# Late picks' last steps on GpSimd, and the first eight row gathers behind their own slots

## The chip, the cores and the metric

The kernel runs on one core of one Trainium2 chip. The metric is the device time of one execution in microseconds (us). TensorE multiplies matrices, VectorE and ScalarE work element by element, GpSimd here issues gathers (DMAs whose rows are chosen by an index in SBUF) and does a little element work, SyncE issues the plain loads. All are ordered only by semaphores.

## The reference

The program is two transformer-like blocks over 256 tokens of width 2048, all in fp32. The change lies in the last part of the second block, a product-key expert layer:

```python
def peer_ffn(h, w_pq, peer_keys, peer_u, peer_v):
    q = jnp.einsum("bsd,dhk->bshk", h, w_pq).reshape(B, S, PEER_HEADS, 2, KEY_DIM)
    sub = jnp.einsum("bshpk,hpnk->bshpn", q, peer_keys).astype(jnp.float32)
    s, i = lax.top_k(sub, PEER_TOPK)                       # 16 best of 128, for two key sets
    cand = (s[..., 0, :, None] + s[..., 1, None, :]).reshape(B, S, PEER_HEADS, PEER_TOPK * PEER_TOPK)
    cidx = (i[..., 0, :, None] * N_KEYS + i[..., 1, None, :]).reshape(...)
    top_s, pos = lax.top_k(cand, PEER_TOPK)                # 16 best of the 256 sums
    idx = jnp.take_along_axis(cidx, pos, axis=-1)          # the experts
    gate = jax.nn.softmax(top_s, axis=-1)
...
        u = jnp.take(peer_u, i_blk, axis=0)
        a = jax.nn.gelu(jnp.einsum("td,thkd->thk", x_blk, u)) * g_blk
        v = jnp.take(peer_v, i_blk, axis=0)
        return jnp.einsum("thk,thkd->td", a, v)
```

There are 8 heads, 16 experts for each token and head, and 16384 experts with a row of 2048 numbers (8 KB) in each of the tables u and v.

## The kernel before

Tokens lie on the 128 partitions, in two halves. A **unit** is one head of one half: 16 units, 16 picks each, so 256 **gathers** in all. A gather fetches for each of 128 tokens one row of u: 128 rows of 8 KB, 1 MB. It lands in one of eight slots (`GR = 8`) of the tile `expert_rows`. For each gather VectorE runs one **dot** (L2195), the product of the row and the normed token `h2`, summed over 2048 elements. Dot n releases slot n % 8 (semaphore `freed`), and GpSimd's gather n + 8 waits for that; so eight gathers at most are issued or landed and not yet used. GpSimd runs its instructions in the order written.

What experts a unit picks is worked out by VectorE in three **parts**, in the list `PICK_PARTS`. `best_keys` finds the 16 best of 128 keys, twice. `best_pairs` finds the 16 best of the 256 sums and splits each position into two places. `experts_of_pairs` (L1776 to L1790) turns places into experts: it compares places with a row of numbers (`one_hot`, 2 x 16 x 16), multiplies by the key numbers `best_f`, sums over the last 16 into `keys_of`, and makes the index, `keys_of[0] * 128 + keys_of[1]`, cast to an integer. Then it increments `picked`, and the gathers of that unit may go.

Units 0 to 3 are picked in the stage before (`out_and_queries_stage`), between VectorE's halves of the weight split (L194). The 12 late units are picked between the dots of the gather stage (`peer_stage`): 36 parts spread over the first 232 dots (`PICK_DOTS`), so one part behind every sixth or seventh dot, and a unit's three parts take 19.33 dots. Third parts stand behind dots 19, 38, 57, 77, 96, 115, 135, 154, 173, 193, 212 and 231; the next part behind them follows 6 dots later in 4 cases (19, 77, 135, 193) and 7 dots later in 7.

The first eight gathers are issued at the end of `out_and_queries_stage`. Slots 0 to 3 lie where the four-slot ring of weight slabs was, slots 4 to 7 where the high and low halves of the split weights were. Behind dot 236 VectorE makes the indices of the next phase (`index_pieces`). When all dots are done, the v phase begins: gathers of half rows of v on one side, and slabs of v multiplied by TensorE on the other. Its first six slab loads (L2107) start when dot 248 is done.

Of the kernel before, what the change touches and what calls it, by code (L numbers as in the profile page):

```python
# [23 lines left out]
ALU = mybir.AluOpType  # L24
AX = mybir.AxisListType

P = 128
# [17 lines left out]
PH, NKEYS, TOPK = 8, 128, 16  # L45
PICKS = PH * TOPK
RING = 4
KPE_W = 256
GR = 8
# [3 lines left out]
C_ID, C_NA, C_CAUSAL, C_TRIL, C_FREQ, C_IOTA = 0, 128, 384, 512, 640, 672  # L53
# [49 lines left out]
class Core:  # L103
# [33 lines left out]
    def place(self, name, shape, dt=F32, at=None):  # L137

        at = self.at if at is None else self.arena + at
        size = 4 * int(np.prod(shape[1:]))  # L140
        self.at = at + (size + 31) // 32 * 32
        return self.nc.alloc_sbuf_tensor_at(name, shape, dt, offset=at)
# [1631 lines left out]
    step.all(v.tensor_copy(b.place_f[:], b.place_u[:]))  # L1774


def experts_of_pairs(core, dve, step, u, sub, b):


    v, wide = core.nc.vector, [P, TOPK, TOPK]  # L1780
    hot = core.const[:, C_IOTA:C_IOTA + TOPK].unsqueeze(1).broadcast_to(wide)
    step.all(*[v.tensor_tensor(b.one_hot[:, s], hot, b.place_f[:, s, :].unsqueeze(2).broadcast_to(wide), ALU.is_equal)
               for s in range(2)])
    step.all(*[v.tensor_tensor(b.one_hot[:, s], b.one_hot[:, s], b.best_f[:, s, :].unsqueeze(1).broadcast_to(wide),  # L1784
                               ALU.mult) for s in range(2)])
    where = slice(u * TOPK, (u + 1) * TOPK)
    step.all(*[v.tensor_reduce(b.keys_of[:, s, where], b.one_hot[:, s], AX.X, ALU.add) for s in range(2)])  # L1787
    step.all(v.scalar_tensor_tensor(out=b.expert_f[:], in0=b.keys_of[:, 0, where], scalar=float(NKEYS),
                                    in1=b.keys_of[:, 1, where], op0=ALU.mult, op1=ALU.add))
    v.tensor_copy(b.index[:, where], b.expert_f[:]).then_inc(b.picked, 1)  # L1790
# [4 lines left out]


PICK_PARTS = (best_keys, best_pairs, experts_of_pairs)
EARLY_UNITS = 4
PICK_DOTS = 232


def gather_row(nc, p, n, peer_u):


    nc.gpsimd.indirect_dma_start(  # L1805
        p.rows[:, n % GR, :], None, peer_u, bass.IndirectOffsetOnAxis(ap=p.index[:, n:n + 1], axis=0)
    ).then_inc(p.landed[n % GR], 16)


def out_and_queries_stage(core, block, w_out, w_queries, gain_rows, keys_in_dram, x_home, peer_u, p):  # L1810
# [9 lines left out]
    nc, base, outs = core.nc, core.tiles, core.outs  # L1820
# [10 lines left out]
    with ExitStack() as local:  # L1831
# [152 lines left out]

        @block.gpsimd
        def _(pool):
            pool.wait_ge(core.slabs_used, (base + 8) * RING + 2)
            pool.wait_ge(p.picked, 1)
            for n in range(GR):
                gather_row(nc, p, n, peer_u)  # L1990

        @block.vector
# [52 lines left out]
def peer_stage(core, block, p, peer_u, peer_v, counts, gain, out):  # L2045
# [15 lines left out]
    UNITS, KB, SLOTS, HALF = NH * PH, 1024, 6, D // 2  # L2061
# [3 lines left out]
    with ExitStack() as local:  # L2065
        core.local = local
        (done, freed, shifted, exped, gelued, weighted, turned, columns, rows_hot, rows_one, hot_used, distant, read,
         iota_in, sums_in, x_back, gain_in, added, sums, mean_ready, rooted, normed, stored, final, piece_used,
         pieces_indexed, slab_used) = core.new(
            "dve_done", "rows_used", "shifted", "exponentiated", "gelued", "weighted", "picks_turned",  # L2070
            "columns_copied", "rows_hot", "rows_one", "hot_used", "distant", "spread_read", "iota_in",
            "sums_in", "x_back", "gain_in", "x_added", "x_sums", "mean_ready", "rooted", "normed",
            "stored", "final_steps", "pieces_used", "pieces_indexed", "expert_slabs_used")
        cols_hot = core.new("cols_hot_low", "cols_hot_high")
        slab_in = core.new(*[f"expert_slab_in{i}" for i in range(SLOTS)])
        piece_landed = core.new(*[f"piece_landed{i}" for i in range(GR)])
# [1 line left out]
        place = core.place  # L2078
# [20 lines left out]
        def half_of(half):  # L2099
            return slice(half * PICKS, (half + 1) * PICKS)  # L2100

        @block.sync
        def _(sp):
            sp.dma_start(iota, counts).then_inc(iota_in, 16)
            for m in range(SLOTS):
                sp.wait_ge(freed, NH * PICKS + m // 2 + 1)
                sp.dma_start(slabs[:, m], v_rows[:, m, 0:HALF]).then_inc(slab_in[m], 16)  # L2107
            sp.wait_ge(freed, NH * PICKS + 4)
            sp.wait_ge(p.x_kept, 16)
            sp.dma_start(summed[:], rows_out[:, :, HALF:D]).then_inc(sums_in, 16)  # L2110
            for m in range(SLOTS, NKEYS):
                sp.wait_ge(slab_used, m - SLOTS + 1)
                sp.dma_start(slabs[:, m % SLOTS], v_rows[:, m, 0:HALF]).then_inc(slab_in[m % SLOTS], 16)
                if m == NKEYS // 2:
                    sp.dma_start(left[:], rows_out[:, :, 0:HALF]).then_inc(x_back, 16)
                    sp.dma_start(gains[:], gain.partition_broadcast(P)).then_inc(gain_in, 16)
            for half in range(NH):
                for part in range(2):
                    at = slice(part * D // 2, (part + 1) * D // 2)
                    sp.wait_ge(normed, 2 * half + part + 1)  # L2120
                    sp.dma_start(rows_out[:, half, at], result[:, half, at]).then_inc(stored, 16)
            sp.wait_ge(stored, 16 * 2 * NH)

        @block.gpsimd
        def _(pool):
            for n in range(GR, UNITS * TOPK):
                if n % TOPK == 0:
                    pool.wait_ge(p.picked, n // TOPK + 1)
                pool.wait_ge(freed, n + 1)
                gather_row(nc, p, n, peer_u)  # L2130
            pool.wait_ge(freed, NH * PICKS + GR)
            pool.wait_ge(pieces_indexed, NH)
            for n in range(UNITS * TOPK):
                if n >= GR:
                    pool.wait_ge(piece_used, n - GR + 1)
                nc.gpsimd.indirect_dma_start(  # L2136
                    pieces[:, n % GR, :], None, v_pieces,
                    bass.IndirectOffsetOnAxis(ap=piece_at[n % NH][:, n // NH:n // NH + 1], axis=0)
                ).then_inc(piece_landed[n % GR], 16)

        @block.vector
        def _(dve):
            step, final_step = Steps(dve, done), Steps(dve, final)
            wide = p.total[:].unsqueeze(2).broadcast_to([P, PH, TOPK])
# [31 lines left out]
            def index_pieces():  # L2176
                step.all(*[nc.vector.scalar_tensor_tensor(out=piece_f[half], in0=p.keys_of[:, 0, half_of(half)], scalar=float(NKEYS),
                                                          in1=p.keys_of[:, 1, half_of(half)], op0=ALU.mult, op1=ALU.add)
                           for half in range(NH)])
                for half in range(NH):  # L2180
                    nc.vector.tensor_scalar(piece_at[half], piece_f[half], 2.0, 1.0, ALU.mult, ALU.add).then_inc(
                        pieces_indexed, 1)
# [2 lines left out]
            nc.vector.memset(core.small[:, 61:62], 0.0).then_inc(hot_used, 8)  # L2185
            nc.vector.memset(core.small[:, 62:63], 0.0).then_inc(read, 2)
            dve.wait_ge(p.scores_out, 2 * 4)
            parts_left = 3 * (UNITS - EARLY_UNITS)
            for u in range(UNITS):
                for j in range(TOPK):  # L2190
                    n = u * TOPK + j
                    dve.wait_ge(landed[n % GR], n // GR * 16 + 16)
                    if n:
                        dve.wait_ge(freed, n + GR - 1)
                    nc.vector.tensor_tensor_reduce(out=junk[:, n % 2, :], in0=rows[:, n % GR, :], in1=p.h2[:, u // PH, :],  # L2195
                                                   scale=1.0, scalar=0.0, op0=ALU.mult, op1=ALU.add,
                                                   accum_out=weight[:, n:n + 1]).then_inc(freed, 1)
                    k = n * parts_left // PICK_DOTS
                    if k < (n + 1) * parts_left // PICK_DOTS and k < parts_left:
                        PICK_PARTS[k % 3](core, dve, step, EARLY_UNITS + k // 3, p.sub, p)  # L2200
                    if n in (4 * TOPK + 6, PICK_DOTS + 1):
                        shift(u // PH)
                    if n in (5 * TOPK + 6, 15 * TOPK + 6):
                        share(u // PH)
                    if j == 2 and u == PH:
                        weigh(0)
                    if n == PICK_DOTS + 4:
                        index_pieces()
            weigh(1)
            dve.wait_ge(iota_in, 16)  # L2210
# [178 lines left out]
def build(nc, ins, out):  # L2389
    with ExitStack() as ctx:  # L2390
        core = Core(nc, ctx)
# [165 lines left out]
        def gate_source(t):  # L2557
# [9 lines left out]
        p = Named()  # L2567
# [5 lines left out]
        p.rows = place("expert_rows", [P, GR, D], at=-112 * KB)  # L2573
        p.best = place("best", [P, 2, TOPK], at=32 * KB)
        (p.best_at, p.rest, p.cand, p.cand_rest, p.best_f, p.top, p.top_at, p.place_u, p.place_f, p.one_hot, p.expert_f,
         p.index, p.total) = (place(*b) for b in (
            ("best_at", [P, 2, TOPK], U32), ("rest", [P, 2, NKEYS]), ("cand", [P, TOPK * TOPK]),
            ("cand_rest", [P, TOPK * TOPK]), ("best_f", [P, 2, TOPK]), ("top", [P, NH * PH, TOPK]),
            ("top_at", [P, TOPK], U32), ("place_u", [P, 2, TOPK], U32), ("place_f", [P, 2, TOPK]),
            ("one_hot", [P, 2, TOPK, TOPK]), ("expert_f", [P, TOPK]), ("index", [P, NH * PICKS], U32),  # L2580
            ("total", [P, PH])))
        p.squares = place("squares", [P, 2, 512], at=44 * KB)
        p.sub = place("key_scores", [P, NH, 2 * PH, NKEYS], at=48 * KB)
        p.h2 = place("h2", [P, NH, D], at=64 * KB)
# [41 lines left out]
```

## Time and profile before

| | us |
|---|---|
| median of 3 runs | 3234.27 (3233.52 to 3235.56) |
| span of the profiled execution | 3233.2 |
| what lies around the span | 1.1 of the median |
| gather stage, first dot's start to last dot's start | 1998.36 to 2675.38 |
| GpSimd busy over the whole span | 823.7 |
| VectorE busy over the whole span | 2188.2 |

The profile is one execution; the span is the time from its first to its last instruction. An instruction's row in the timeline gives its start, its length and, in brackets, how long its engine stood idle ahead of it and what released it. A row that ends in x2 is two instructions run together, its length that of both.

### The profile page before, as it was taken

To read this page: it belongs to the slowest core of one execution; us is meant where nothing else is said; L and a number is where in the kernel's file an instruction comes from. 1 tells how busy PE (TensorE), PEld (TensorE's weight loads), DVE (VectorE), ACT (ScalarE), POOL (GpSimd) and SP (SyncE) were. 2 spreads that over 40 slices of the span, in tenths; PEclk is the share of its full clock that TensorE was granted. 3 is DMA by queue.
4 is the path that set the end of the run, shared out by engine and by line. 5 is a ranking of instruction groups with operands and counts; after the bars stand their busy time and mean duration, and the time that the engine had idled before them with its cause. 6 is when DMAs were issued, how large, how long until landed. Compare 5 with 4: busy or idle time off the path is not lost. (4 is left out here: it accounts for less than half of the span.)

```text
span 3233.2 us, 30451 instructions
## 1 busy us (share of the span) xinstructions
PE 2442.6 (76%) x10473; PEld 1867.0 (58%) x10473; DVE 2188.2 (68%) x3036; ACT 1107.1 (34%) x1880; POOL 823.7 (25%) x571
## 2 busy tenths in 40 slices
PE   6896999999999999999999996000034005999994
PEld 5765787888888887888778796000023004444441
DVE  3698546545454555564545558999999999565668
ACT  4434235344343445454555442000089105000000
POOL 0200000000010100000000002777766773644444
PEclk9998599999999999999999998555555558999997
DMA  8452065565656555655435564999999996999998
GB/s 241 156 169 91 7 203 176 189 195 183 193 184 194 181 195 173 201 172 176 153 122 183 175 213 185 420 397 386 393 394 394 389 404 217 376 409 410 409 409 344
DMA packets 277587, 813.19 MB, mean 252 GB/s; under 512 B 32601, under 2 KB 40001, under 8 KB 243424
## 3 DMA queue, kind: packets, MB, share of 16 engines
q1 hardware_dynamic: 203504, 408.87, 37.9%
q0 software_dynamic: 73728, 402.69, 31.4%
q8 instruction: 63, 1.03, 0.1%
q14 instruction: 52, 0.43, 0.0%
q10 hardware_dynamic: 240, 0.18, 0.0%
HBM read 807.48 MB, written 4.19 MB: 251 GB/s over the span
## 5 line engine op out<-in xcount | busy, mean ns | idle before, releaser
L194 DVE TENSOR_TENSOR wl<-ring,wh 128x1024 fp32r<-128x1024 f32 (+2 forms) x616 | 738.9, 1241 | 647.1 <-ACT wh L189 644.5
L189 ACT CAST wh<-ring 128x1024 fp32r<-128x1024 f32 (+2 forms) x616 | 609.7, 1040 | 702.7 <-PE ps L210 649.1
L208 PE MATMUL ps<-wh,th 128*128 128x512 f32 (+1 forms) x1632 | 641.5, 393 | 28.8 <-DVE wl L194 21.6
L1805 POOL DMA_INDIRECT expert_rows<-in_peer_u,index x256 | 481.7, 1882 | 626.7 <-PE ps L1891 437.8
L210 PE MATMUL ps<-wh,tl 128*128 128x512 f32 (+1 forms) x1632 | 634.4, 389 | 0.0
L209 PE MATMUL ps<-wl,th 128*128 128x512 f32 (+1 forms) x1632 | 634.3, 389 | 0.0
L2195 DVE CUSTOM_DVE_ANT_0 junk<-expert_rows,h 128x2048 f32<-128x2048 f32 x256 | 570.1, 2287 | 6.0 <-DMA expert_rows<-in_peer_u,index 5.1
L2218 DVE SCALAR_TENSOR_TENSOR x_and_pieces<-expert_pieces,const,x_and_pieces 128x1024 f32<-128x1024 f32 x256 | 327.8, 1283 | 170.1 <-DMA expert_pieces<-in_peer_v,piece_index 87.2
L2278 PE MATMUL ps<-expert_slabs,by_expert 128*128 128x512 f32 x1024 | 439.7, 592 | 0.7 <-ACT by_expert L2319 0.7
L208 PEld LDWEIGHTS ps<-wh,th 128*128 128x128 f32 x1632 | 308.0, 189 | 101.8 <-DVE wl L194 31.8
L210 PEld LDWEIGHTS ps<-wh,tl 128*128 128x128 f32 x1632 | 307.7, 189 | 63.6
L209 PEld LDWEIGHTS ps<-wl,th 128*128 128x128 f32 x1632 | 308.1, 189 | 60.9
L2278 PEld LDWEIGHTS ps<-expert_slabs,by_expert 128*128 128x128 f32 x1024 | 194.5, 190 | 245.3 <-issue 244.4
L2260 PE MATMUL ps<-const,keys_of 128*128 128x128 f32 x4 | 1.4, 448 | 316.1 <-DVE index L1790 316.1
L1142 POOL TENSOR_TENSOR square<-relu 128x512 f32<-128x512 f32 x32 | 48.4, 1535 | 675.6 <-ACT relu L1097 675.6
L2271 PE MATMUL ps<-col_hot,row_hot 128*128 128x128 f32 x512 | 103.9, 374 | 130.3 <-ACT row_hot L2314 102.0
L208 PE MATMUL ps<-wh,fh 128*128 128x512 f32 x512 | 199.5, 390 | 0.0
L210 PE MATMUL ps<-wh,fl 128*128 128x512 f32 x512 | 199.2, 389 | 0.0
L209 PE MATMUL ps<-wl,fh 128*128 128x512 f32 x512 | 199.2, 389 | 0.0
L2260 PEld LDWEIGHTS ps<-const,keys_of 128*128 128x128 f32 x4 | 0.6, 204 | 316.6 <-DVE index L1790 316.6
L2271 PEld LDWEIGHTS ps<-col_hot,row_hot 128*128 128x128 f32 x512 | 91.8, 272 | 142.5 <-ACT col_hot L2308 57.7
L2136 POOL DMA_INDIRECT expert_pieces<-in_peer_v,piece_index x128 | 133.8, 1045 | 142.0 <-DVE x_and_pieces L2218 127.6
(332 smaller groups left out, 2748.5 us busy)
## 6 DMA issues: line engine op xcount, KB each, us to landing
ring<-in_w_in SPq DMA_DIRECT2D x112, 1024.0 KB, 5.1
ring<-in_w_up SPq DMA_DIRECT2D x64, 1024.0 KB, 5.3
ring<-in_w_down SPq DMA_DIRECT2D x64, 1024.0 KB, 5.0
expert_slabs<-in_peer_v SPq DMA_DIRECT2D x128, 512.0 KB, 6.8
ring<-in_w_out SPq DMA_DIRECT2D x32, 1024.0 KB, 5.0
ring<-in_w_peer_q SPq DMA_DIRECT2D x16, 1024.0 KB, 5.2
ring<-in_w_ukv SPq DMA_DIRECT2D x8, 1024.0 KB, 5.3
ring<-in_w_uq SPq DMA_DIRECT2D x8, 768.0 KB, 4.6
```

Source lines behind the costliest of these rows:

```text
L189: self.nc.scalar.copy(self.wh[:, i % 2, two, 0:w], self.ring[:, i, two, 0:w]).then_inc(self.high_ready, 1)
L194: self.nc.vector.tensor_tensor(self.wl[:, i % 2, two, 0:w], self.ring[:, i, two, 0:w], self.wh[:, i % 2, two, 0:w].bitcast(F32), ALU.subtr ...
L208: mm(o, hi, wh, start=start and k == 0, stop=False)
L209: mm(o, hi, wl, start=False, stop=False)
L210: last = mm(o, lo, wh, start=False, stop=stop and k == 3)
L1142: nc.gpsimd.tensor_tensor(square[:, n % 2, half, :], r, r, ALU.mult).then_inc(squared, 1)
L1805: nc.gpsimd.indirect_dma_start(p.rows[:, n % GR, :], None, peer_u, bass.IndirectOffsetOnAxis(ap=p.index[:, n:n + 1], axis=0)).then_inc(p.l ...
L2136: nc.gpsimd.indirect_dma_start(pieces[:, n % GR, :], None, v_pieces, bass.IndirectOffsetOnAxis(ap=piece_at[n % NH][:, n // NH:n // NH + 1] ...
L2195: nc.vector.tensor_tensor_reduce(out=junk[:, n % 2, :], in0=rows[:, n % GR, :], in1=p.h2[:, u // PH, :], scale=1.0, scalar=0.0, op0=ALU.mu ...
L2218: nc.vector.scalar_tensor_tensor(out=summed[:, half, :], in0=pieces[:, n % GR, :], scalar=weight[:, c:c + 1], in1=summed[:, half, :], op0= ...
L2271: mm(core.ps[:, 4 + i // 4, i % 4 * P:(i % 4 + 1) * P], row_hot[:, i, :], col_hot[:, i, :], start=True, stop=True).then_inc(hot_used, 1)
L2278: end = mm(core.ps[:, 2 * half + q, :], by_expert[:, half, m, :], slabs[:, m % SLOTS, q * 512:(q + 1) * 512], start=m == 0, stop=m == NKEY ...
```

## The change

There are two edits. First, the third part of a late unit becomes `places_of_pairs`: VectorE makes `one_hot` and a copy of `best_f` (`best_kept`), and increments `places_hot`. GpSimd does the rest (`keys_by_pool`): two multiplications of 256 elements a partition, four additions that fold 16 numbers to one (256, 128, 64 and 32 elements), and three instructions of 16 elements for the index. Each but the second multiplication waits for the one before. They stand in GpSimd's order behind the gather with the same place in the count, 8 later than the dot. VectorE waits for `picked` ahead of the next `places_of_pairs` and ahead of `index_pieces`. Second, the first eight gathers no longer wait for the last product of the weight stage: 0 to 3 wait until VectorE has split the slab in their slot, 4 to 7 until TensorE has used the split half in theirs.

```diff
+def places_of_pairs(core, dve, step, u, sub, b):
+    v, wide = core.nc.vector, [P, TOPK, TOPK]
+    hot = core.const[:, C_IOTA:C_IOTA + TOPK].unsqueeze(1).broadcast_to(wide)
+    step.all(*[v.tensor_tensor(b.one_hot[:, s], hot, b.place_f[:, s, :].unsqueeze(2).broadcast_to(wide), ALU.is_equal)
+               for s in range(2)])
+    v.tensor_copy(b.best_kept[:], b.best_f[:]).then_inc(b.places_hot, 1)
+
+def keys_by_pool(core, pool, step, u, b):
+    g, wide = core.nc.gpsimd, [P, TOPK, TOPK]
+    where = slice(u * TOPK, (u + 1) * TOPK)
+    pool.wait_ge(b.places_hot, u - EARLY_UNITS + 1)
+    step.all(*[g.tensor_tensor(b.one_hot[:, s], b.one_hot[:, s], b.best_kept[:, s, :].unsqueeze(1).broadcast_to(wide), ALU.mult)
+               for s in range(2)])
+    for n in (8, 4, 2):
+        step(g.tensor_tensor(b.one_hot[:, :, :, 0:n], b.one_hot[:, :, :, 0:n], b.one_hot[:, :, :, n:2 * n], ALU.add))
+    step(g.tensor_tensor(b.keys_of[:, :, where], b.one_hot[:, :, :, 0], b.one_hot[:, :, :, 1], ALU.add))
+    step(g.tensor_scalar(b.expert_f[:], b.keys_of[:, 0, where], float(NKEYS), None, ALU.mult))
+    step(g.tensor_tensor(b.expert_f[:], b.expert_f[:], b.keys_of[:, 1, where], ALU.add))
+    g.tensor_copy(b.index[:, where], b.expert_f[:]).then_inc(b.picked, 1)
...
+LATE_PARTS = (best_keys, best_pairs, places_of_pairs)
...
-            pool.wait_ge(core.slabs_used, (base + 8) * RING + 2)
             pool.wait_ge(p.picked, 1)
             for n in range(GR):
+                if n < RING:
+                    pool.wait_ge(core.low_ready, (base + 7) * (2 * RING) + (2 * n + 2))
+                else:
+                    pool.wait_ge(core.slabs_used, (base + 7) * RING + (RING + 1 + n % 2))
                 gather_row(nc, p, n, peer_u)
...
+        parts_left = 3 * (UNITS - EARLY_UNITS)
+
+        def part_at(n):
+            k = n * parts_left // PICK_DOTS
+            return k if k < (n + 1) * parts_left // PICK_DOTS and k < parts_left else None
...
                 pool.wait_ge(freed, n + 1)
                 gather_row(nc, p, n, peer_u)
+                k = part_at(n - GR)
+                if k is not None and k % 3 == 2:
+                    keys_by_pool(core, pool, key_step, EARLY_UNITS + k // 3, p)
...
-                    k = n * parts_left // PICK_DOTS
-                    if k < (n + 1) * parts_left // PICK_DOTS and k < parts_left:
-                        PICK_PARTS[k % 3](core, dve, step, EARLY_UNITS + k // 3, p.sub, p)
+                    k = part_at(n)
+                    if k is not None:
+                        if k % 3 == 2 and k > 3:
+                            dve.wait_ge(p.picked, EARLY_UNITS + k // 3)
+                        LATE_PARTS[k % 3](core, dve, step, EARLY_UNITS + k // 3, p.sub, p)
...
                     if n == PICK_DOTS + 4:
+                        dve.wait_ge(p.picked, UNITS)
                         index_pieces()
```

VectorE's order at the third part of a late unit, before. L2195 is a dot (its second row reads the sum out), and L1782 to L1790 are `experts_of_pairs`:

```order
L2195 ISA const 128x1
L1782 TENSOR_TENSOR one_hot<-const,place_f 128x256 x2
L1784 TENSOR_TENSOR one_hot<-one_hot,best_f 128x256 x2
L1787 TENSOR_REDUCE keys_of<-one_hot 128x16 x2
L1788 SCALAR_TENSOR_TENSOR expert_f<-keys_of 128x16
L1790 CAST index<-expert_f 128x16
L2195 ISA junk,const<-expert_rows,h_12453 128x2048
```

And of the change, where the dot is L2235:

```order
L2235 ISA const 128x1
L1782 TENSOR_TENSOR one_hot<-const,place_f 128x256 x2
L1784 COPY best_kept<-best_f 128x32
L2235 ISA junk,const<-expert_rows,h_12454 128x2048
L2235 ISA const 128x1
```

Six instructions have left VectorE between the two dots, and one has come.

GpSimd's order in the same stage before: the gathers of u (L1805) with nothing between them, then those of v (L2136).

```order
L1805 DMA expert_rows<-in_peer_u,index 128x2048 x8
L2124 UNCONDITIONAL_BRANCH
L1805 DMA expert_rows<-in_peer_u,index 128x2048 x248
L2136 DMA expert_pieces<-in_peer_v,const 128x1024
L2136 DMA expert_pieces<-in_peer_v,piece_index 128x1024
```

And of the change, where the gather is L1832 and L1793 to L1800 are `keys_by_pool`:

```order
L1832 DMA expert_rows<-in_peer_u,index 128x2048 x8
L2161 UNCONDITIONAL_BRANCH
L1832 DMA expert_rows<-in_peer_u,index 128x2048 x20
L1793 TENSOR_TENSOR one_hot<-one_hot,best_kept 128x256 x2
L1796 TENSOR_TENSOR one_hot<-one_hot 128x32x8
L1796 TENSOR_TENSOR one_hot<-one_hot 128x32x4
L1796 TENSOR_TENSOR one_hot<-one_hot 128x32x2
L1797 TENSOR_TENSOR keys_of<-one_hot 128x2x16
L1798 ISA
L1798 TENSOR_SCALAR expert_f<-keys_of 128x16
L1799 TENSOR_TENSOR expert_f<-expert_f,keys_of 128x16
L1800 CAST index<-expert_f 128x16
```

Nine instructions stand between gather 27 and gather 28, and nine again behind every 19 or 20 gathers; what is behind them on GpSimd is a gather each time. The row L1798 ISA stands there only the first time.

## Rows read from the trace of the kernel before

**Rows 1.** The page: its head, and VectorE's costliest group.
```profile
span 3233.2 us, 30451 instructions
...
L2195 DVE CUSTOM_DVE_ANT_0 junk<-expert_rows,h 128x2048 f32<-128x2048 f32 x256 | 570.1, 2287 | 6.0 <-DMA expert_rows<-in_peer_u,index 5.1
```

**Rows 2.** Windows: us, busy us (x instructions) by engine, clock, DMA share, GB/s.
```profile
2100.00:2200.00 100.00, 0.00 (x0) 0.00 (x0) 99.00 (x151) 0.31 (x1) 70.27 (x38) 0.50 0.99 396
```

**Rows 3.** Timeline, VectorE: start us, us, work, [idle before it].
```profile
1998.36 2.29 DVE L2195 CUSTOM_DVE_ANT_0 junk<-expert_rows,h 128x2048 f32<-128x2048 f32 x1 [2.68 <-DMA expert_rows<-in_peer_u,index]
...
2002.12 2.29 DVE L2195 CUSTOM_DVE_ANT_0 junk<-expert_rows,h 128x2048 f32<-128x2048 f32 x1 [1.46 <-DMA expert_rows<-in_peer_u,index]
...
2004.62 2.29 DVE L2195 CUSTOM_DVE_ANT_0 junk<-expert_rows,h 128x2048 f32<-128x2048 f32 x1 [0.20 <-DMA expert_rows<-in_peer_u,index]
...
2016.81 0.48 DVE L1753 MAX8 best<-key_scores 128x8 f32<-128x128 f32 x2
...
2020.00 2.29 DVE L2195 CUSTOM_DVE_ANT_0 junk<-expert_rows,h 128x2048 f32<-128x2048 f32 x1
...
2049.51 2.29 DVE L2195 CUSTOM_DVE_ANT_0 junk<-expert_rows,h 128x2048 f32<-128x2048 f32 x1
...
2617.38 2.28 DVE L2195 CUSTOM_DVE_ANT_0 junk<-expert_rows,h 128x2048 f32<-128x2048 f32 x1
...
2675.38 2.28 DVE L2195 CUSTOM_DVE_ANT_0 junk<-expert_rows,h 128x2048 f32<-128x2048 f32 x1
```

**Rows 4.** Timeline, GpSimd, three gathers.
```profile
1992.38 1.14 POOL L1805 DMA_INDIRECT expert_rows<-in_peer_u,index  x1 [437.84 <-PE ps L1891]
...
2199.34 1.91 POOL L1805 DMA_INDIRECT expert_rows<-in_peer_u,index  x1 [0.30 <-issue]
...
2224.16 0.94 POOL L1805 DMA_INDIRECT expert_rows<-in_peer_u,index  x1 [0.30 <-issue]
```

**Rows 5.** Timeline, VectorE, two dots and two parts of a pick.
```profile
2198.15 2.28 DVE L2195 CUSTOM_DVE_ANT_0 junk<-expert_rows,h 128x2048 f32<-128x2048 f32 x1
...
2200.36 2.28 DVE L2195 CUSTOM_DVE_ANT_0 junk<-expert_rows,h 128x2048 f32<-128x2048 f32 x1
...
2207.00 0.76 DVE L1782 TENSOR_TENSOR one_hot<-const,place_f 128x256 f32<-128x256 f32 x2
...
2207.79 0.76 DVE L1784 TENSOR_TENSOR one_hot<-one_hot,best_f 128x256 f32<-128x256 f32 x2
...
2209.69 2.29 DVE L2195 CUSTOM_DVE_ANT_0 junk<-expert_rows,h 128x2048 f32<-128x2048 f32 x1
...
2242.54 0.17 DVE L1767 CAST best_f<-best_at 128x32 f32<-128x32 uint32 x1
...
2245.49 2.29 DVE L2195 CUSTOM_DVE_ANT_0 junk<-expert_rows,h 128x2048 f32<-128x2048 f32 x1
```

**Rows 6.** Timeline, GpSimd and VectorE in earlier stages.
```profile
1080.74 1.04 POOL L1142 TENSOR_TENSOR square<-relu 128x512 f32<-128x512 f32 x1 [19.63 <-ACT relu L1097]
...
1080.74 3.02 POOL L1142 TENSOR_TENSOR square<-relu 128x512 f32<-128x512 f32 x2 [19.63 <-ACT relu L1097]
...
1081.63 3.21 DVE L194 TENSOR_TENSOR wl<-ring,wh 128x1024 fp32r<-128x1024 f32 x2 [4.18 <-ACT wh L189]
...
1956.99 2.36 DVE L194 TENSOR_TENSOR wl<-ring,wh 128x1024 fp32r<-128x1024 f32 x2 [2.18 <-ACT wh L189]
...
81.85 1.29 POOL L2429 TENSOR_TENSOR biases<-biases,const 128x512 f32<-128x512 f32 x1 [1.83 <-PE ps L210]
```

**Rows 7.** Issues and queues: one group, median us from issue to landing.
```profile
expert_rows<-in_peer_u,index POOLq DMA_INDIRECT x256, 9.9
```

**Rows 8.** Timeline: VectorE's last weight split, ScalarE's last scores, SyncE's first slabs.
```profile
1981.81 2.36 DVE L194 TENSOR_TENSOR wl<-ring,wh 128x1024 fp32r<-128x1024 f32 x2 [2.35 <-ACT wh L189]
...
1994.50 1.52 ACT L1960 ACTIVATE key_scores<-ps,small 128x512 f32<-128x512 f32 x2 [1.31 <-PE ps L1903]
...
2662.21 5.23 SPq L2107 DMA_DIRECT2D expert_slabs<-in_peer_v  x6
```

More of the change, by code:

```diff
@@ L2068, in peer_stage @@
          iota_in, sums_in, x_back, gain_in, added, sums, mean_ready, rooted, normed, stored, final, piece_used,
-         pieces_indexed, slab_used) = core.new(
+         pieces_indexed, slab_used, key_steps, p.places_hot) = core.new(
             "dve_done", "rows_used", "shifted", "exponentiated", "gelued", "weighted", "picks_turned",
@@ L2072, in peer_stage @@
             "sums_in", "x_back", "gain_in", "x_added", "x_sums", "mean_ready", "rooted", "normed",
-            "stored", "final_steps", "pieces_used", "pieces_indexed", "expert_slabs_used")
+            "stored", "final_steps", "pieces_used", "pieces_indexed", "expert_slabs_used",
+            "key_steps", "places_hot")
         cols_hot = core.new("cols_hot_low", "cols_hot_high")
@@ L2125, in _ @@
         def _(pool):
+            key_step = Steps(pool, key_steps)
             for n in range(GR, UNITS * TOPK):
@@ L2187, in _ @@
             dve.wait_ge(p.scores_out, 2 * 4)
-            parts_left = 3 * (UNITS - EARLY_UNITS)
             for u in range(UNITS):
@@ L2575, in build @@
         (p.best_at, p.rest, p.cand, p.cand_rest, p.best_f, p.top, p.top_at, p.place_u, p.place_f, p.one_hot, p.expert_f,
-         p.index, p.total) = (place(*b) for b in (
+         p.index, p.total, p.best_kept) = (place(*b) for b in (
             ("best_at", [P, 2, TOPK], U32), ("rest", [P, 2, NKEYS]), ("cand", [P, TOPK * TOPK]),
@@ L2580, in build @@
             ("one_hot", [P, 2, TOPK, TOPK]), ("expert_f", [P, TOPK]), ("index", [P, NH * PICKS], U32),
-            ("total", [P, PH])))
+            ("total", [P, PH]), ("best_kept", [P, 2, TOPK])))
         p.squares = place("squares", [P, 2, 512], at=44 * KB)
```

## The prediction

> **What bounds the kernel now.** I read the page first, for where the time is, then the busy time by windows, then the timeline of VectorE, then GpSimd's beside it. In the gather stage VectorE is busy 99.00 of 100 us while the DMA queues are also at a share of 0.99, with 396 GB/s [rows 2]. Two resources near their limits mean that I must know both paces. VectorE's: dots follow each other by 2.21 us (2198.15, 2200.36) [rows 5]. The queues': at the start of the stage each dot waits for its row (idle 2.68, 1.46, 0.20 us), and from the second landing to the third is 2.50 us (2002.12 to 2004.62) [rows 3]. So bare dots would outrun the gathers, 2.21 against 2.50, and only the picks, during which VectorE asks for no rows, leave the queues time. Of its idle time VectorE spends 5.1 us in all on gathers [rows 1], and 4.34 of it is ahead of the three dots shown; afterwards VectorE is the bound. From dot 19 (2049.51) to dot 231 (2617.38) are 11 whole units: 567.9 / 11 = 51.6 us each [rows 3]. A unit checks: 19.33 dots x 2.21 = 42.8, `best_keys` 3.19 (2016.81 to 2020.00), `best_pairs` 2.95 (2242.54 to 2245.49), the third part 2.69 (2207.00 to 2209.69), together 51.6 [rows 3, 5]. The queues need 19.33 x 2.50 = 48.3 us of a unit. A saving on VectorE can be had only down to that.
>
> **What VectorE saves.** What stays of the third part is the comparison, 0.79 us (2207.00 to 2207.79) [rows 5], and a copy, for which I take 0.12, below the 0.17 of a cast of the same size [rows 5]: 0.91, so 1.78 us less in a unit. Without any return that is 12 x 1.78 = 21 us.
>
> **What GpSimd's instructions meet.** The trace has no gather stage with element work on GpSimd, but it shows how the two engines meet. A gather alone takes 0.94 us (2224.16, beside `best_keys`), and 1.91 among dots [rows 4]: that of 2199.34 starts during the dot of 2198.15 and ends at 2201.25, 0.89 behind the start of the next dot at 2200.36. It did its work only once the dot was over. In the MLP two GpSimd squares take 1.04 and 1.98 us (3.02 for both) and VectorE's two splits started beside them take 3.21 instead of 2.36 [rows 6]: the second square waited for the first split, and the second split waited 0.85 us for the square. So work on GpSimd that reads SBUF and VectorE's work with two inputs exclude each other for whole instructions, and they alternate. The Trainium skill says the same (SBUF — State Buffer, Who interferes with whom): the pair of ports shared by GpSimd and VectorE is an exclusive lock, and a VectorE instruction with two SBUF inputs contends with a GpSimd instruction that reads SBUF. By that rule, the trace agrees. Its consequence speaks against this change: a dot has two SBUF inputs, so each of the nine instructions waits for a dot to end.
>
> **One unit, worked out.** Sizes first. A two-input GpSimd instruction of 512 elements takes 1.29 us [rows 6]; with a floor of 0.1 (an estimate, between nothing and the 0.94 of a gather) and the rest in proportion: 0.70 for 256 elements, 0.40 for 128, 0.25 for 64, 0.2 for the last four. Bounds: 0.65 (pure proportion) and 1.04 (the square's whole time) for the large ones. A square of 1.04 held VectorE 0.85, so one holds it its length less 0.19: 3 x 0.51 + 0.21 + 0.06 = 1.8 us in a unit. That alone takes back all that VectorE saves.
>
> Then the wait. Let dot m be the one with the third part, time 0 its end. GpSimd issues gather m+8 and comes to its nine instructions about when VectorE has done its 0.91 us and started dot m+1. One instruction goes at the end of each dot. Where the next part follows 6 dots later, VectorE reaches it at 0.91 + 6 x 2.21 + 1.8 = 16.0; five instructions are done by then. Beside `best_keys` the other four go without waiting, 0.2 each and 0.30 between [rows 4], by 18.0. Gather m+9 is issued by 19.2 (0.30 + 0.94). A first gather on quiet queues took from 1993.52, its issue's end, to the dot's start at 1998.36, 4.8 us [rows 3, 4]; so row m+9 is there at 24.0. The queues do not cover this: rows land 9.9 us after their issue [rows 7], up to 2.50 x 6 = 15 with six on their way, and the last one ahead of the gap was issued at about 1.3. VectorE has used its last landed row at 16.0 + 3.19 + 2 x 2.21 = 23.6, and waits. Where 7 dots lie between, the same sum gives 18.2, 19.7, 20.9, 25.7, and VectorE runs dry at 23.6 too. All eight slots are then empty at once, and the queues set the pace: the next row 3.8 us later, as at the start (1998.36 to 2002.12), then 2.50 each. From row m+9's landing, dot m+13 starts 3.8 + 3 x 2.50 = 11.3 later and ends at 13.5, `best_pairs` takes 2.95 to 16.5, the other 6.33 dots run at 2.21: 30.5 us. A unit is 24.0 + 30.5 = 54.5 in 4 cases and 56.2 in 7, mean 55.6, against 51.6: +4.0, times 11 = +44.
>
> **The ends.** Start: with slots 0 to 3 free by 1984.2 (the last split) [rows 8], their gathers land ahead of the stage; dot 0 can go at 1996.0 when ScalarE has the last scores (1994.50 + 1.52) [rows 8], and seven dots end at 2011.5 instead of 2016.81 [rows 3]: -5.3. No more is to be had there, as VectorE had no other idle time. End: from dot 231's end (2619.59) to the last dot's (2677.59) are 58.0 now [rows 3]. Changed: 0.91 + 5 dots 11.1 + held 1.7 = 13.7 to dot 236; GpSimd's last five instructions (0.25, and four at 0.2 + 0.30) bring the wait for `picked` to 16.0; gather 240 follows at 17.2, lands at 22.0, the next 3.8 later, 14 more at 2.50, the last dot 2.2: 63.0. The first slab loads of v (6 x 512 KB, started at dot 248 [rows 8]) now meet a full queue: 3.1 MB at 1 MB in 2.50 are 7.5 us, of which I put half, 3.8, ahead of the last rows. So 66.8, +8.8. What follows the last dot moves with it.
>
> Sum: 3233.2 - 5.3 + 44 + 8.8 = 3280.7; with the 1.1 us around the span, 3282.
>
> **Rivals.** (A) Faster: GpSimd's element work runs beside the dots as if it were a plain issue, and holds nothing. Then the nine take 3.55 us and eight gaps of 0.3, 6 us, less than the 9.9 a row is on its way, and no row is late: 11 x -1.78 - 5.3 - 1.8 = -27, time 3207. It decides once an instruction needs no dot's end. For it: the dots' pitch is 2.21 whether a gather lies among them or not. Against it: the squares. Chance 0.12. (B) The lock holds, but GpSimd keeps it from one instruction to the next: the keys are done behind one dot, VectorE is held 3.55 us (the nine) to 6 us (with the gaps) against 1.78 saved, no row is late: +1.8 to +4.2 a unit. At 1.8, 12 times, with the start, +16: 3250. Against it: the splits and squares alternated. Chance 0.10. (C) The nine are dearer: large ones 1.04, small ones 0.5, or something at each turn from gather to element work. Each us of delay to gather m+9 is 12 us of time. 2.5 to 6 us give 3312 to 3354. The Trainium skill (GPSIMD Engine Reference, 2.1) puts about 6 us on the first call of a freshly loaded kernel; at each of 12 turns that would be this case's upper end. The trace's first gather started without such a gap that I can see, and nothing here alternates the two. Chance 0.15. (D) Savings and holds cancel and the slots cover the wait: within 0.2% (6.5 us), which is about what a measurement of this kernel can tell from no change. Chance 0.06. My forecast has the remaining 0.57, its own range 3258 to 3312: the landing that follows the first at 2.50 instead of 3.8 takes 16 off, and large instructions at 1.04 add some 15 to 30.
>
> **The numbers.** Faster 0.13 (A and a little), same 0.06, slower 0.81. The range reaches from 3228 (A left out, D in) to 3325 (the dearer half of C out): about 0.8.
>
> **What the changed profile would show.** Right: GpSimd's rows L1793 to L1796 with a mean near 2 us where rows of half the size of the squares cost 0.7 alone, each ending 0.5 to 0.9 behind the start of a dot; about 18 us from gather m+8 to m+9; VectorE waiting on the gather once a unit for 0.5 to 3 us and by 0.2 to 0.3 per dot for the next few; DMA share of the stage down from 0.99 to about 0.9; dot 0 at about 1996; the v phase as long as before. Wrong: rows L1793 near 0.7 us and a unit of 50 us (A), or a run of nine behind one dot (B), or gaps of microseconds ahead of the first multiplication (C). The forecast fails most easily in the time between dot m and gather m+9, since all else hangs on it.

## The result

The changed kernel takes 3275.57 us (median of 4 runs, 3272.62 to 3277.63) against 3233.89 us (4 runs) of the kernel before in the same session. The ratio is 1.0126, with a 95% interval of 1.0112 to 1.0141: 1.3% slower.

The page of the changed kernel, its head and the two costliest groups of the gather stage, GpSimd's gathers and VectorE's dots, to be read against [rows 1]:

```profile
span 3275.1 us, 30501 instructions
...
L1832 POOL DMA_INDIRECT expert_rows<-in_peer_u,index x256 | 480.0, 1875 | 517.0 <-DVE wl L194 426.8
L2235 DVE CUSTOM_DVE_ANT_0 junk<-expert_rows,h 128x2048 f32<-128x2048 f32 x256 | 594.4, 2364 | 47.2 <-DMA expert_rows<-in_peer_u,index 45.9
```

VectorE waits 45.9 us for rows instead of 5.1, and its dots have a mean of 2364 ns instead of 2287, which is 19.7 us over all 256. (The busy times of the dots differ by 24.3 us. Dots that follow each other at once overlap by 0.08 us in the profile, and dots that wait do not.)

VectorE's timeline gives the stage's marks: dot 0, dot 19, dot 231 and the last dot (start us, us, work, idle before it), against [rows 3].

```profile
1994.90 2.29 DVE L2235 CUSTOM_DVE_ANT_0 junk<-expert_rows,h 128x2048 f32<-128x2048 f32 x1 [0.28 <-ACT key_scores L1987]
...
2043.09 2.29 DVE L2235 CUSTOM_DVE_ANT_0 junk<-expert_rows,h 128x2048 f32<-128x2048 f32 x1
...
2652.58 2.29 DVE L2235 CUSTOM_DVE_ANT_0 junk<-expert_rows,h 128x2048 f32<-128x2048 f32 x1
...
2721.49 2.29 DVE L2235 CUSTOM_DVE_ANT_0 junk<-expert_rows,h 128x2048 f32<-128x2048 f32 x1 [1.48 <-DMA expert_rows<-in_peer_u,index]
```

Four numbers add up to the whole difference of the spans, 41.9 us. Up to dot 19: 2043.09 against 2049.51, -6.4. The 11 units to dot 231: 609.5 / 11 = 55.41 us each against 51.6, +41.6. From dot 231 to the last: 68.9 against 58.0, +10.9. Behind the last dot: 3275.1 - 2721.5 = 553.6 against 557.8, -4.2.

GpSimd's timeline through one unit shows where a unit's time goes. The dot with this unit's third part (dot 77) ends at 2210.73.

```profile
2211.92 2.83 POOL L1832 DMA_INDIRECT expert_rows<-in_peer_u,index  x1 [0.30 <-issue]
2215.05 1.90 POOL L1832 DMA_INDIRECT expert_rows<-in_peer_u,index  x1 [0.30 <-issue]
2216.96 4.71 POOL L1793 TENSOR_TENSOR one_hot<-one_hot,best_kept 128x256 f32<-128x256 f32 x2
2221.75 5.47 POOL L1796 TENSOR_TENSOR one_hot<-one_hot 128x256 f32<-128x256 f32 x3
2227.30 0.24 POOL L1797 TENSOR_TENSOR keys_of<-one_hot 128x32 f32<-128x32 f32 x1
...
2228.25 0.20 POOL L1800 CAST index<-expert_f 128x16 uint32<-128x16 f32 x1
2228.60 1.02 POOL L1832 DMA_INDIRECT expert_rows<-in_peer_u,index  x1 [0.15 <-issue]
```

And VectorE's beside it:

```profile
2218.28 2.80 DVE L2235 CUSTOM_DVE_ANT_0 junk<-expert_rows,h 128x2048 f32<-128x2048 f32 x1
...
2221.02 2.80 DVE L2235 CUSTOM_DVE_ANT_0 junk<-expert_rows,h 128x2048 f32<-128x2048 f32 x1
...
2223.75 2.79 DVE L2235 CUSTOM_DVE_ANT_0 junk<-expert_rows,h 128x2048 f32<-128x2048 f32 x1
...
2226.48 0.48 DVE L1753 MAX8 best<-key_scores 128x8 f32<-128x128 f32 x2
...
2240.53 2.29 DVE L2235 CUSTOM_DVE_ANT_0 junk<-expert_rows,h 128x2048 f32<-128x2048 f32 x1 [0.84 <-DMA expert_rows<-in_peer_u,index]
```

The first four instructions of GpSimd, the two multiplications and two additions, take 9.9 us, one for each dot's end; the five behind them, beside `best_keys`, 1.5. The 12 units have four, five or six such waits each, 59 in all. Three dots are held: they and what follows start 2.74 us apart where 2.21 is free running, 1.6 us in the unit. From dot 77's end to the end of the issue of the gather behind the nine (gather 86) are 18.9 us. Then dots wait for rows.

### The profile page after: what moved, and what is told of

It is laid out like the page before. It is cut to its first block and busy times, and to the rows that moved or that the text cites. A ratio compares the mean times of both kernels' runs of the same rounds, so it can differ in the third digit from the quotient of the medians.

```text
span 3275.1 us, 30501 instructions
## 1 busy us (share of the span) xinstructions
PE 2443.3 (75%) x10473; PEld 1865.9 (57%) x10473; DVE 2193.9 (67%) x2976; ACT 1107.1 (34%) x1880; POOL 973.4 (30%) x679
## 5 line engine op out<-in xcount | busy, mean ns | idle before, releaser
L1832 POOL DMA_INDIRECT expert_rows<-in_peer_u,index x256 | 480.0, 1875 | 517.0 <-DVE wl L194 426.8
L2235 DVE CUSTOM_DVE_ANT_0 junk<-expert_rows,h 128x2048 f32<-128x2048 f32 x256 | 594.4, 2364 | 47.2 <-DMA expert_rows<-in_peer_u,index 45.9
L2177 POOL DMA_INDIRECT expert_pieces<-in_peer_v,const x128 | 127.6, 997 | 147.1 <-DVE x_and_pieces L2261 123.6
```

What stands on the lines that cost most here:

```text
L1832: nc.gpsimd.indirect_dma_start(p.rows[:, n % GR, :], None, peer_u, bass.IndirectOffsetOnAxis(ap=p.index[:, n:n + 1], axis=0)).then_inc(p.l ...
L2177: nc.gpsimd.indirect_dma_start(pieces[:, n % GR, :], None, v_pieces, bass.IndirectOffsetOnAxis(ap=piece_at[n % NH][:, n // NH:n // NH + 1] ...
```

## The experiments

Ten kernels were run. Their times are medians, and "before" is the kernel before, run beside them on the same chip (3233.93 to 3234.29 us). First, each edit by itself.

**The early gathers alone.** Only this is changed:

```diff
-            pool.wait_ge(core.slabs_used, (base + 8) * RING + 2)
             pool.wait_ge(p.picked, 1)
             for n in range(GR):
+                if n < RING:
+                    pool.wait_ge(core.low_ready, (base + 7) * (2 * RING) + (2 * n + 2))
+                else:
+                    pool.wait_ge(core.slabs_used, (base + 7) * RING + (RING + 1 + n % 2))
```

> Only the second edit (the first eight gathers wait for their slots); all picks wholly on VectorE as before. In the changed kernel dot 0 starts at 1994.90 and dot 19 at 2043.09, against 1998.36 and 2049.51, so both my theories give 6.4 us less up to dot 19, and none of it given back, since VectorE waits for no row afterwards: 3227 to 3229. A rival is that the v phase, which is bound by transfers at its end, gives it back: then 3231 to 3234.

3228.33 us, ratio 0.9983 (0.9974 to 0.9992): 5.6 us faster, as both said, and nothing given back. This is the base for what follows.

**GpSimd's keys alone**, the first gathers waiting as before.

```diff
+            pool.wait_ge(core.slabs_used, (base + 8) * RING + 2)
             pool.wait_ge(p.picked, 1)
             for n in range(GR):
-                if n < RING:
...
```

> Only the first edit (GpSimd makes the late units' keys), the first gathers wait as before. Theory (rows come late because nine instructions in a row keep the gathers back) and rival (VectorE's dots are held) both give the changed kernel plus the 6.4 us of the early gathers: 3280 to 3284. If the reserve of landed rows from the early gathers matters more than that, above 3284.

3276.58 us, ratio 1.0134 (1.0118 to 1.0149). That is a miss: 1 us more than the changed kernel, not 6.4. With GpSimd's keys in place an early start is worth next to nothing. The dots show where it is lost: dot 19 starts at 2047.88, 4.8 us later than in the changed kernel, dot 77 is still 5.0 later, dot 135 2.3, and from dot 212 (0.3 earlier) to the last (2720.58, 0.9 earlier) nothing is left. So the lead is given back in the middle of the stage, in steps. Why, no kernel here tests, and it stays open.

**Nine spare instructions.** VectorE does the late picks itself; GpSimd does the nine on tiles of their own.

```diff
+def experts_and_signal(core, dve, step, u, sub, b):
+    experts_of_pairs(core, dve, step, u, sub, b)
+    core.nc.vector.tensor_copy(b.best_kept[:], b.best_f[:]).then_inc(b.places_hot, 1)
...
-LATE_PARTS = (best_keys, best_pairs, places_of_pairs)
+LATE_PARTS = (best_keys, best_pairs, experts_and_signal)
...
-    step.all(*[g.tensor_tensor(b.one_hot[:, s], b.one_hot[:, s], b.best_kept[:, s, :]...
+    step.all(*[g.tensor_tensor(b.s_hot[:, s], b.s_hot[:, s], b.best_kept[:, s, :]...
...
```

> The late picks wholly on VectorE as before, early gathers kept; GpSimd does the same nine instructions on spare tiles, whose result nobody uses, at the same place and behind the same signal (VectorE also makes the copy best_kept). Theory (the nine keep the gathers back, the eight slots run empty, rows come late): nearly the whole loss is there though VectorE has lost nothing but 1.6 us of holds in a unit, so 3272 to 3296, VectorE waiting some 30 to 46 us for rows. Rival (the loss is the time that dots are held): 3228 + 12 x 1.6 + 2 = 3249, VectorE waiting under 5 us for rows.

3295.99 us, ratio 1.0196 (1.0181 to 1.0212); VectorE waits 38.6 us for rows. So the nine cost 3296 - 3228.3 = 67.7 us. The changed kernel is 3296 - 3275.6 = 20.4 us faster than this one, close to what VectorE should save, 12 x 1.78 = 21. Both kernels wait for rows, so the difference is no clean measure of the saving; it only agrees with it.

**The same nine as memsets.**

```diff
-    step.all(*[g.tensor_tensor(b.s_hot[:, s], b.s_hot[:, s], b.best_kept[:, s, :]...
+    step.all(*[g.memset(b.s_hot[:, s], 0.0) for s in range(2)])
+    step(g.memset(b.s_hot[:, 0], 0.0))
     for n in (8, 4, 2):
-        step(g.tensor_tensor(b.s_hot[:, :, :, 0:n], b.s_hot[:, :, :, 0:n], b.s_hot[:, :, :, n:2 * n], ALU.add))
...
+        step(g.memset(b.s_hot[:, 0, :, 0:n], 0.0))
+    step(g.memset(b.s_f[:], 0.0))
+    step(g.memset(b.s_f[:], 0.0))
+    g.memset(b.s_f[:], 0.0).then_inc(b.spare, 1)
```

> As the kernel with nine spare instructions, but all nine are memsets of the same sizes, which only write SBUF; nobody uses what they write. Theory (an instruction that reads SBUF waits for the end of a dot, one that only writes does not): the nine pass in 2 to 3 us, no row is late, 3228 to 3234. Rival (any element instruction of GpSimd takes a turn at a dot's end, or the queue order and the semaphore waits between the nine cost the time): 3260 to 3296.

3229.36 us, ratio 0.9985 (0.9975 to 0.9994): free but for the copy. GpSimd's timeline in this kernel:

```profile
2203.89 0.56 POOL L1793 MEMSET s_hot<- 128x256 f32 x2 [0.53 <-DVE best_kept L1827]
2204.51 0.31 POOL L1794 MEMSET s_hot<- 128x256 f32 x1
2204.88 0.60 POOL L1796 MEMSET s_hot<- 128x128 f32 x3
2205.53 0.11 POOL L1797 MEMSET s_f<- 128x16 f32 x1
2205.70 0.11 POOL L1798 MEMSET s_f<- 128x16 f32 x1
2205.87 0.11 POOL L1799 MEMSET s_f<- 128x16 f32 x1
```

And the dot beside them:

```profile
2203.74 2.29 DVE L2242 CUSTOM_DVE_ANT_0 junk<-expert_rows,h 128x2048 f32<-128x2048 f32 x1
```

All nine pass within one dot. Position, signal, count and the semaphore waits between them are the same as in the kernel with nine reading instructions; what is gone is reading SBUF, and the arithmetic with it. The next kernel has reads with next to no arithmetic. The Trainium skill, page "SBUF — State Buffer", section "Who interferes with whom", says that two-input VectorE work contends with GpSimd instructions that read SBUF and not with ones that only write; these two kernels agree, at 67.7 us against 1.0.

**Nine short reads**: all nine are copies of 16 elements.

```diff
-    step.all(*[g.tensor_tensor(b.one_hot[:, s], b.one_hot[:, s], b.best_kept[:, s, :]...
...
+    for _ in range(8):
+        step(g.tensor_copy(b.s_i[:], b.s_f[:]))
+    g.tensor_copy(b.s_i[:], b.s_f[:]).then_inc(b.spare, 1)
```

> As the kernel with nine spare instructions, but all nine are copies of 16 elements, each behind the one before; nobody uses them. Short ones held no dot in the traces so far. Theory (late rows, not holds, are the loss): nine turns at a pitch of 2.21 without the 1.6 us of holds, so 66 - 12 x 1.6 = 47 us of the 66 remain, 3228 + 1.4 + 47 = 3277, from 3265 to 3285. Rival (holds are what counts): 3230 to 3235.

3276.55 us, ratio 1.0123 (1.0108 to 1.0139). The dots' mean length is 2289 ns, that of before: none is held. The page's groups for the copies, and a stretch of GpSimd's timeline:

```profile
L1794 POOL CAST s_i<-s_f 128x16 uint32<-128x16 f32 x96 | 169.1, 1762 | 9.6 <-DVE best_kept L1823 4.3
L1795 POOL CAST s_i<-s_f 128x16 uint32<-128x16 f32 x12 | 2.4, 197 | 0.8
```

```profile
2217.24 13.77 POOL L1794 CAST s_i<-s_f 128x16 uint32<-128x16 f32 x8 [0.54 <-DVE best_kept L1823]
2231.07 0.20 POOL L1795 CAST s_i<-s_f 128x16 uint32<-128x16 f32 x1
```

A copy that takes 0.20 us when no dot runs takes 1.76 on average. Waiting alone costs 3276.6 - 3229.4 = 47 us. Between this kernel and the one with nine full instructions lie 19.4 us, as much as the holds, 12 x 1.6. So as far as these two show, waits and holds add up and neither hides the other.

**One instruction between gathers.** Here I put to the test why rows are late. The prediction had it that nine in a row make one gap which the eight slots can't cover. `keys_one_by_one` is `keys_by_pool` as a generator, which hands back after each instruction.

```diff
                 if k is not None and k % 3 == 2:
-                    keys_by_pool(core, pool, key_step, EARLY_UNITS + k // 3, p)
+                    if k // 3 < 9:
+                        spread_keys = keys_one_by_one(core, pool, key_step, EARLY_UNITS + k // 3, p)
+                    else:
+                        keys_by_pool(core, pool, key_step, EARLY_UNITS + k // 3, p)
+                if spread_keys is not None and next(spread_keys, 0) == 0:
+                    spread_keys = None
```

> As the changed kernel, but for the first nine late units one of the nine instructions stands behind each of nine gathers in place of nine in a row; the last three units as in the changed kernel. Theory (the long gap between two gathers empties the eight slots): no gap, so these nine units cost only their holds, about as much as VectorE saves: 3275 - 9 x 5 = 3230 to 3245. Rival (GpSimd's turns are the budget: 28.3 instructions a unit and one turn for each dot's end, with a few more in the parts): as late as before, 3268 to 3282.

3272.84 us, ratio 1.0114 (1.0098 to 1.0129). My theory of the gap falls. Spread over nine gathers, the same instructions cost about the same, and VectorE waits 44.7 us for rows, in 83 waits instead of 63. What is left is the rival, the number of turns: GpSimd finishes one reading instruction or one gather at each dot's end, a unit has 19.33 gathers and 9 others, and only beside VectorE's one-input parts, or while VectorE waits, can it do more.

**Six short reads** tests the budget by its size.

```diff
-    for _ in range(8):
+    for _ in range(5):
         step(g.tensor_copy(b.s_i[:], b.s_f[:]))
```

> As the kernel with nine short spare copies, but six a unit. Theory now (GpSimd has a budget of turns: 19.33 gathers a unit, one turn for each dot's end, and about 4 more, the 94 us that it idles behind VectorE in the kernel with memsets, over 12 units and 2.21 us): 6 - 4 turns too many a unit against 9 - 4 for nine, so 2/5 of 47 us: 3249, from 3240 to 3256. Rival (a gap that the eight slots cover costs nothing, and six turns of 2.21 are 13 us, near what a row takes to land): 3228 to 3233.

3251.65 us, ratio 1.0054 (1.0037 to 1.0071), VectorE waiting 21.2 us for rows. The rival of a covered gap is out, and the budget was within 3 us. GpSimd's own waits say where the spare turns come from. In the kernel with memsets, while gathers of u are issued:

```profile
POOL expert_rows L1838 <- DVE const L2242: 94.0, 37, 4.1
```

and in the changed kernel:

```profile
POOL expert_rows L1832 <- DVE const L2235: 9.9, 3, 3.6
```

(us in total, times, longest.) The three waits of the changed kernel are ahead of gathers 8, 15 and 21; from the first late unit on, GpSimd no longer waits for a slot to come free. Nor are the queues the bound of the whole stage: from 2050 to 2600 us their share is 0.89, where it was 0.99.

The budget says where the cost begins, and not how steep it is. 94 us in 12 units are 3.5 turns, and the two costs, 22.3 us for six copies and 47.2 for nine, fit 3.3 (22.3 to 47.2 is as 6 - 3.3 to 9 - 3.3). But 36 copies more cost 24.9 us, 0.69 each and not a turn of 2.21; the expectation took its slope from the kernel with nine. A likely reason is in the traces: while VectorE waits for a row, no dot holds GpSimd up. Of the 228 gathers from gather 28 on, 74 take under 1.3 us in the kernel with nine short reads, 68 with six and 35 with memsets. The slope isn't worked out from this. Nor does the budget explain the early start: if GpSimd's list alone set the pace from the first late unit on, a lead of 4.8 us should last.

**Three on GpSimd**, the index alone; VectorE multiplies and sums in `places_of_pairs`, and `keys_by_pool` keeps its last three instructions.

```diff
-    v.tensor_copy(b.best_kept[:], b.best_f[:]).then_inc(b.places_hot, 1)
+    step.all(*[v.tensor_tensor(b.one_hot[:, s], b.one_hot[:, s], b.best_f[:, s, :]...
+    for s in range(2):
+        v.tensor_reduce(b.keys_of[:, s, where], b.one_hot[:, s], AX.X, ALU.add).then_inc(b.places_hot, 1)
```

> As the changed kernel, but VectorE also multiplies and sums, and GpSimd has only the last three instructions of 16 elements a unit. Theory (nine turns outlast what eight slots cover, three do not; short ones hold no dot): no row is late, VectorE saves the 0.38 us of two short instructions a unit: 3222 to 3228. Rival (the loss is in proportion to the instructions, 66 us for nine in the kernel with spare instructions): 3228 + 22 - 5 = 3245.

3224.15 us, ratio 0.9969 (0.9957 to 0.9981): 4 us under the early gathers alone. Three turns are within the budget: the unit from dot 19 to dot 38 takes 50.45 us where it took 50.89. Only the last three dots wait for rows, 3.3 us together, beside the first slab loads of v.

**Keys in two windows.** GpSimd's instructions stand where VectorE runs no dots, for the first eight late units; the last four are VectorE's.

```diff
+                k = part_at(n - (GR - 2))
+                if k is not None and 3 <= k < 3 * WINDOW_UNITS + 3 and k % 3 == 0:
+                    pool.wait_ge(freed, GR + n - (GR - 2) + 1)
+                    products_by_pool(core, pool, key_step, EARLY_UNITS + k // 3 - 1, p)
+                if k is not None and 4 <= k < 3 * WINDOW_UNITS + 3 and k % 3 == 1:
+                    pool.wait_ge(freed, GR + n - (GR - 2) + 1)
+                    index_by_pool(core, pool, key_step, EARLY_UNITS + k // 3 - 1, p)
...
-                        LATE_PARTS[k % 3](core, dve, step, EARLY_UNITS + k // 3, p.sub, p)
+                        (LATE_PARTS if k // 3 < WINDOW_UNITS else PICK_PARTS)[k % 3](core, dve, step, EARLY_UNITS + k // 3, p.sub, p)
```

Here `products_by_pool` is the two multiplications and the first addition, `index_by_pool` the other six.

> As the changed kernel, but for the first eight late units GpSimd's nine instructions stand where VectorE has one-input work and no dots: the two multiplications and the first addition behind the dot ahead of the next unit's best_keys, the other six behind the dot ahead of its best_pairs, each after a wait for that dot. The last four units are picked wholly by VectorE. Theory (the loss comes of instructions that wait for the ends of dots): hardly one waits, no row is late, and VectorE keeps its 1.78 us in each of eight units: 3228 - 14 + 2 for a few holds = 3212 to 3218. Rival (a row of instructions between gathers costs wherever it stands, since GpSimd loses the time in which it catches up): 3228 to 3255.

3214.89 us, ratio 0.9939 (0.9926 to 0.9953): 0.6% faster than before and 60 us under the changed kernel, with the same nine instructions on GpSimd, though in eight late units and not in twelve. Its GpSimd rows:

```profile
2208.79 1.41 POOL L1794 TENSOR_TENSOR one_hot<-one_hot,best_kept 128x256 f32<-128x256 f32 x2 [1.49 <-DVE const L2247]
2210.28 0.72 POOL L1796 TENSOR_TENSOR one_hot<-one_hot 128x256 f32<-128x256 f32 x1
2211.27 0.98 POOL L1840 DMA_INDIRECT expert_rows<-in_peer_u,index  x1 [0.27 <-POOL one_hot L1796]
...
2228.35 0.82 POOL L1804 TENSOR_TENSOR one_hot<-one_hot 128x128 f32<-128x128 f32 x2 [1.49 <-DVE const L2247]
2229.25 0.24 POOL L1805 TENSOR_TENSOR keys_of<-one_hot 128x32 f32<-128x32 f32 x1
```

Two multiplications take 1.41 us here and 4.71 in the changed kernel. No dot is held (mean 2288 ns), and VectorE waits for no row. The queues are busy throughout now, share 1.00 at 402 GB/s from 2050 to 2600 us, so there is little left to save on VectorE.

**All nine in one window**, ten units.

```diff
-                k = part_at(n - GR)
-                if k is not None and k % 3 == 2:
-                    keys_by_pool(core, pool, key_step, EARLY_UNITS + k // 3, p)
+                k = part_at(n - (GR - 2))
+                if k is not None and 3 <= k < 3 * WINDOW_UNITS + 3 and k % 3 == 0:
+                    pool.wait_ge(freed, GR + n - (GR - 2) + 1)
+                    keys_by_pool(core, pool, key_step, EARLY_UNITS + k // 3 - 1, p)
...
```

> As the kernel with the keys in two windows, but all nine instructions stand in one, beside the next unit's best_keys, for ten late units in place of eight; the last two are picked wholly by VectorE. Five or six of the nine fit beside the 3.19 us of best_keys, so three or four must wait for dots, within the budget of 4 turns. Theory: no row is late, 3228 - 10 x 1.78 = 3210, from 3208 to 3214. Rival (what waits for a dot delays gathers that are then missed, or GpSimd no longer catches up): 3220 to 3240.

3275.37 us, ratio 1.0123 (1.0106 to 1.0140): as slow as the changed kernel, and my expectation missed by 65 us. One window:

```profile
2230.93 1.65 POOL L1796 TENSOR_TENSOR one_hot<-one_hot,best_kept 128x256 f32<-128x256 f32 x2
2232.66 7.41 POOL L1799 TENSOR_TENSOR one_hot<-one_hot 128x256 f32<-128x256 f32 x3
...
2240.89 2.21 POOL L1802 TENSOR_TENSOR expert_f<-expert_f,keys_of 128x16 f32<-128x16 f32 x1
2243.16 2.13 POOL L1803 CAST index<-expert_f 128x16 uint32<-128x16 f32 x1
```

`best_keys` runs from 2228.79 to 2232.04 in this kernel. GpSimd comes to its nine 2.1 us late, so only the multiplications fall in the window; the rest takes turns again and holds dots (2.69, 2.79, 2.52). My count had left out that a window filled with keys is no longer there for catching up with gathers, and that a GpSimd that is behind misses the next window too. The trace shows the order of the two. The first window is entered on time, 0.17 us behind the start of `best_keys`; five instructions fit and four take dots' turns, as counted; and the second is entered 0.91 us late, the third and fourth 2.1. Only three of the ten are entered on time. How much of the cost is each one's, no kernel here tells.

## Why the prediction was right

The direction, the mechanism of waiting for dots' ends and the size (3282 forecast, 3275.6 measured) held; the step from late gathers to late rows did not, and that its number came out is in part luck.

- **What VectorE saves**, 1.78 us a unit: the kernel with nine spare instructions agrees, with 20.4 us for 12 units. Where no row is late it shows cleanly: with two windows a unit from dot 19 to dot 38 takes 49.1 us instead of 50.89.
- **What GpSimd's instructions meet**: as read from [rows 4, 6]. The memsets show it.
- **The sizes.** 0.70 us for 256 elements: two take 1.41 in the kernel with two windows. 0.40 and 0.25 for 128 and 64: the two together are 0.82 there, with the pause between them, a little more than forecast.
- **The holds**, 1.8 us a unit forecast, are 1.6: three dots by 0.53. I had five instructions holding and one per dot from dot m+1 on. In the unit shown GpSimd still has two gathers to issue when dot m ends, its first multiplication starts 6.2 us later (2216.96 against 2210.73), and five of the nine fall beside `best_keys`.
- **The time to the next gather**, 19.2 us forecast for a unit with 6 dots between its parts, is 18.9. That is luck: the gap between gather m+8 and gather m+9 was forecast at about 18 us and is 13.6 (2215.05 to 2228.60). Gather m+8 is issued late and fewer of the nine wait, and the two errors cancel.
- **The step that failed** is the one behind it, "All eight slots are then empty at once, and the queues set the pace". Late rows were put down to one long gap that the slots don't cover. The nine spread between gathers cost about as much (3272.8), and six cost 22 us where a covered gap would be free: GpSimd's turns are the budget, some 3.5 spare ones a unit. A unit of 55.6 us was forecast and 55.41 measured, but the budget as it stands gives no time of its own for nine in a row, so that the forecast's number came so close is not explained by it. For the spread kernel the gap's account was wrong by 28 us or more (3230 to 3245 expected).
- **The start**, -5.3 forecast, is -6.4 in this kernel, and as an edit by itself -5.6. But as part of this change it is worth 1 us. The forecast simply added it, and that was a second, smaller fault.
- **The end**: +8.8 forecast from dot 231 on, +10.9 measured. VectorE waits 1.4 us for the last unit's keys, forecast 2.3. The last rows do meet the slabs' loads, which start at 2701.04 in the changed kernel: its last four dots, behind that, wait 1.46 to 1.50 us each for a row.
- **Behind the last dot**: no change forecast, -4.2 measured. VectorE's first piece of v starts 5.1 us behind the last dot's end (2728.76 against 2723.70) where it was 8.5 (2686.09 against 2677.59), presumably since the slabs' loads started 20.5 us ahead of the last dot's start (2701.04) and not 13.2 (2662.21). The trace fits: GpSimd issues the first piece's gather 0.35 us behind the last dot in both, and the sixth slab has landed by then in the changed kernel only.
- **What the profile should show.** Rows L1793 have a mean of 2.3 us, the queues' share is 0.89, VectorE waits for rows once in most units, at first by 0.8 to 2.2 us a dot and then by 0.2, and dot 0 starts at 1994.90: as forecast. The gap of 18 us is the sign that failed.
- **The rivals.** A (nothing waits) is what the memsets do. B (GpSimd keeps its place) and C (a price at each turn from gathers to element work) are not seen: the two multiplications in a row alternate with dots, and the first one follows its gather at once.

## What to carry to other kernels

Before work is moved to GpSimd to relieve VectorE, look at what VectorE runs beside it. Beside long instructions with two SBUF inputs, each GpSimd instruction that reads SBUF takes a whole turn, the time from one end to the next (2.21 us here, for a copy that alone takes 0.20), and long ones hold VectorE as well. If GpSimd also issues the gathers on which VectorE lives, its spare turns are the budget, and its idle time behind VectorE in the profile says roughly how many there are: 94 us in the kernel with memsets and 120.8 in the kernel before are 3.5 and 4.6 turns a unit, where the costs fit 3.3. Its busy share (70% of this stage) does not, as much of that was waiting: a gather takes 1.91 us among dots and 0.94 beside `best_keys`.

The same nine instructions were worth -13 us in eight units, placed in VectorE's one-input stretches, and +47 us in twelve units where the change put them, both against the early gathers alone. A window must be entered on time, and it has to leave room for what it was used for before.

## What the runs showed of the hardware

A memset of 256 elements on GpSimd passes at 0.31 us beside a running dot, and a copy of 16 elements waits for the dot's end, 1.76 us on average. Of GpSimd's instructions that did get their turn, multiplications of 256 elements delayed the next dot (by 0.53 us, for 0.72 of their own), and the copies of 16 elements didn't delay it measurably (dots' mean 2289 ns), nor do gathers: dots follow each other by 2.21 us with a gather among them, which ends 0.9 us into the next dot.
